# Seven-product units: eleven of the FFN's 22 input units instead of eight, in pairs, with the block sums kept in SBUF

## The reference

```
h = rmsnorm(x, norm_ffn)
gt, up = split(h @ w_ffn_in, 2)        # w_ffn_in: 1024 x 5632, D_FF = 2816
x = x + (silu(gt) * up) @ w_ffn_out    # w_ffn_out: 2816 x 1024
return rmsnorm(x, norm_final)
```

## Time and profile before

| | |
|---|---|
| time, median of three runs | 794.04 us (792.46 to 794.29) |
| the profiled execution's own time | 792.53 us |
| its span in the profile | 790.7 us |
| PE busy | 782.2 us, 99% |
| DVE, ACT, POOL busy | 457.6, 309.4, 105.3 us |
| TensorE clock granted | 0.998 of full speed |

### The profile page before, as it was taken

How to read it: one execution, slowest core, us unless ns; L and a number is a source line. 1 busy time by engine, 2 the same in 40 slices (tenths; PEclk the granted TensorE clock), 3 DMA queues, 4 the chain that set the end, 5 groups by cost and what they waited for, 6 DMA issues and landing times.

```text
span 790.7 us, 11974 instructions
## 1 busy us (share of the span) xinstructions
PE 782.2 (99%) x4670; PEld 666.1 (84%) x4670; DVE 457.6 (58%) x895; ACT 309.4 (39%) x552; POOL 105.3 (13%) x75
## 2 busy tenths in 40 slices
PE   9999999999999999999999999999999999999996
PEld 7878899889878787788888888999999998888885
DVE  5935432645766876657527698666666655422347
ACT  6212155243646566642316352333323323222235
POOL 1301000000000000002200671433333300000000
PEclk9999999999999999999999999999999999999999
DMA  7931345340311111145331533333333334222202
GB/s 236 346 121 54 107 93 148 73 122 4 108 54 54 54 54 42 41 146 145 134 109 75 139 106 107 107 106 106 106 106 105 93 127 155 106 107 106 106 1 106
DMA packets 101274, 83.32 MB, mean 105 GB/s; under 512 B 16960, under 2 KB 94832, under 8 KB 101232
## 3 DMA queue, kind: packets, MB, share of 16 engines
q1 hardware_dynamic: 100992, 82.46, 34.9%
q10 hardware_dynamic: 240, 0.29, 0.1%
HBM read 77.44 MB, written 5.29 MB: 105 GB/s over the span
## 4 chain that ended last, share of the span: by engine, by line
PE 98%; DMA 0%; ACT 0%; issue 0%; DVE 0%; ACTq 0%; DVEq 0%
PE bank L1699 28%; PE bank L1700 28%; PE bank L1701 28%; PE bank L1932 2%; PE bank L1951 2%; PE bank L1919 2%; PE bank L1833 1%; PE bank L1874 1%; PE bank L1855 1%; PE bank L1796 1%; PE bank L1740 1%; PE bank L1946 1%; PE bank L1746 0%; PE bank L1749 0%; PE bank L1723 0%; PE bank L1886 0%
## 5 line engine op out<-in xcount | busy, mean ns | idle before, releaser
L1023 DVE TENSOR_TENSOR w_lo<-w_raw,w_hi 128x2048 fp32r<-128x2048 f32 (+2 forms) x29 | 64.5, 2225 | 79.8 <-ACT w_hi L660 79.8
L1699 PE MATMUL bank<-n_hi,w_hi 128*128 128x512 f32 x272 | 108.8, 400 | 0.0
L1701 PE MATMUL bank<-n_hi,w_lo 128*128 128x512 f32 x272 | 106.1, 390 | 0.0
L1700 PE MATMUL bank<-n_lo,w_hi 128*128 128x512 f32 x272 | 106.0, 390 | 0.0
L1699 PE MATMUL bank<-h_hi,w_hi 128*128 128x512 f32 (+1 forms) x272 | 99.5, 366 | 0.8 <-issue 0.8
L1700 PE MATMUL bank<-h_lo,w_hi 128*128 128x512 f32 (+1 forms) x272 | 99.1, 364 | 0.0
L1701 PE MATMUL bank<-h_hi,w_lo 128*128 128x512 f32 (+1 forms) x272 | 99.0, 364 | 0.0
L660 ACT CAST w_hi<-w_raw 128x2048 fp32r<-128x2048 f32 (+2 forms) x29 | 53.6, 1848 | 61.8 <-PE bank L1701 51.0
L1699 PE MATMUL bank<-w_hi,a_hi 128*128 128x512 f32 (+1 forms) x180 | 69.2, 385 | 0.0
L1700 PE MATMUL bank<-w_lo,a_hi 128*128 128x512 f32 (+1 forms) x180 | 69.2, 384 | 0.0
L1701 PE MATMUL bank<-w_hi,a_lo 128*128 128x512 f32 (+1 forms) x180 | 69.2, 384 | 0.0
(11 more groups left out here) (287 smaller groups left out, 1598.8 us busy)
## 6 DMA issues: line engine op xcount, KB each, us to landing
w_raw<-in_w_ffn_in_dram SPq DMA_DIRECT2D x44, 512.0 KB, 5.1
w_raw<-in_w_in_dram SPq DMA_DIRECT2D x37, 512.0 KB, 4.8
w_raw<-in_w_ffn_out_dram SPq DMA_DIRECT2D x22, 512.0 KB, 3.7
w_raw<-in_w_out_dram SPq DMA_DIRECT2D x8, 512.0 KB, 3.7
w_raw<-in_w_in_dram SPq DMA_DIRECT2D x12, 256.0 KB, 4.5
xs<-in_x_dram SPq DMA_DIRECT2D x4, 512.0 KB, 4.9
wck_k<-in_w_ck_dram SPq DMA_DIRECT2D x1, 2048.0 KB, 11.9
wck_v<-in_w_cv_dram SPq DMA_DIRECT2D x1, 2048.0 KB, 13.6
```

What stands on the lines that cost most here:

```text
L1023: dve.tensor_tensor(wlo[u % 2][:, 0:n], raw[u % 2][:, 0:n], whi[u % 2][:, 0:n].bitcast(F32), ALU.subtract).then_inc(lo_done, 1)
L1699: pe.matmul(dst, w[0], x_[0], start=start, stop=False)
L1700: pe.matmul(dst, w[0], x_[1], start=False, stop=False)
L1701: return pe.matmul(dst, w[1], x_[0], start=False, stop=stop)
```

## The change

- Seven units are now 5, 6, 8, 9, 11, 12, 14, 15, 17, 18, 20: eleven in place of eight, two and then one plain unit, in both slots. The loops are written out, unit by unit; `sevens(u)` and `plains(u)` count what came before u, and `multiplied(u)` is the semaphore and count of "unit u has been multiplied".
- There are two sets of `wa`/`wa22` tiles and two `s7` tiles, one per slot. The `s7` tiles now lie where `wlo` of the same slot lies, and `slo7` overwrites `s7` in place. So POOL may write the sums of unit u only when PE is through with the low part of unit u - 2: all of it where u - 2 is plain, and product by product (M5, M6, M7) where it is a seven unit.
- Odd units use banks 4 to 7, even units 0 to 3. The tanh is written into the unit's first bank, and the `gate_mul` instruction reads it there.
- In a seven unit PE begins with the three products of plain blocks; then come the four of sums. One of the seven DVE additions (`early_sums`) and its bank change with this, and the last addition moves to the next unit's `scaled_gate`.
- The t sums on POOL begin after the low part of unit 2. The reload of x waits for the last of the eleven seven units. The output product begins with the tiles of banks 0 to 3.

The core of the diff:

```
-SEVEN_FROM = 5
-SEVEN_N = (FT - 1 - SEVEN_FROM) // 2
+SEVEN = (5, 6, 8, 9, 11, 12, 14, 15, 17, 18, 20)
...
-        s7 = at("weight_sums", [4, 4, P], G + 4608)
+        s7 = [at(f"weight_sums{j}", [4, 4, P], B + 4 * SLOT * (4 + j)) for j in range(2)]
...
+        def multiplied(u):
+
+            return (m_done, 7 * sevens(u) + 7) if u in SEVEN else (gu_ready, plains(u) + 2)
...
             pool.wait_ge(h_lo, 2 * TT)
-            pool.wait_ge(r_ready, 2)
+            pool.wait_ge(lo_done, U_IN + 3)
...
-            def weight_sums(i, begins=False):
-
-                pool.wait_ge(raw_full[1], i * 32 + raw_count(U_IN + SEVEN_FROM))
-                if not begins:
-                    pool.wait_ge(lo_done, i * 2 + (U_IN + SEVEN_FROM - 1))
...
+            for u in SEVEN:
+                k, s = sevens(u), u % 2
+                w = slot_view(raw, s, KC, 256)
+                pool.wait_ge(raw_full[s], raw_count(U_IN + u))
+                if u - 2 in SEVEN:
+                    pool.wait_ge(m_done, 7 * sevens(u - 2) + 5)
+                else:
+                    pool.wait_ge(*multiplied(u - 2))
+                pool.tensor_tensor(s7[s][:, 2], w[:, 0:4, 0:P], w[:, 0:4, P:256], ALU.subtract).then_inc(s_sums, 1)
+                if u - 2 in SEVEN:
+                    pool.wait_ge(m_done, 7 * sevens(u - 2) + 6)
+                pool.tensor_tensor(s7[s][:, 0], w[:, 0:4, P:256], w[:, 4:8, P:256], ALU.add).then_inc(s_sums, 1)
+                pool.wait_ge(s_sums, 4 * k + 2)
+                pool.tensor_tensor(s7[s][:, 1], s7[s][:, 0], w[:, 0:4, 0:P], ALU.subtract).then_inc(s_sums, 1)
+                pool.wait_ge(*multiplied(u - 2))
+                pool.wait_ge(s_sums, 4 * k + 3)
+                pool.tensor_tensor(s7[s][:, 3], w[:, 4:8, 0:P], s7[s][:, 1], ALU.subtract).then_inc(s_sums, 1)
...
+            def keep_m1(u):
+                k = sevens(u)
+                act.wait_ge(m_done, 7 * k + 1)
+                if k:
+                    act.wait_ge(u_sums, 7 * k - 5)
+                act.copy(m1s[:], ps[4 * (u % 2)][:, 0:256]).then_inc(m1_out, 1)
+
+            def tanh_gate(u):
+                s = u % 2
+                act.wait_ge(g_scaled, u + 1)
+                act.activation(ps[4 * s][:], gs[:, s, :], ACT.Tanh, scale=0.5).then_inc(gu_tanh, 1)
...
+            for u in range(4, FT):
+                if u + 1 in SEVEN:
+                    plain_hi(u + 1)
+                tanh_gate(u - 1)
+                if u in SEVEN:
+                    keep_m1(u)
+                if u + 1 in SEVEN:
+                    sums_hi(u + 1)
+                else:
+                    unit_hi(u + 1)
...
+            def early_sums(u):
+
+                k, a = sevens(u), 4 * (u % 2)
+                dve.wait_ge(m1_out, k + 1)
+                dve.wait_ge(m_done, 7 * k + 3)
+                dve.tensor_tensor(gs[:, u % 2, 0:256], ps[a][:, 256:512], m1s[:], ALU.add).then_inc(u_sums, 1)
+                dve.wait_ge(m_done, 7 * k + 4)
+                dve.tensor_tensor(u2s[:], ps[a + 1][:, 0:256], m1s[:], ALU.add).then_inc(u_sums, 1)
...
+            for u in range(4, FT):
+                scaled_gate(u - 1)
+                if u + 1 in SEVEN:
+                    plain_lo(u + 1)
+                gated(u - 1)
+                if u in SEVEN:
+                    early_sums(u)
+                if u + 1 in SEVEN:
+                    sums_lo(u + 1)
+                else:
+                    unit_lo(u + 1)
+                if u in SEVEN:
+                    late_sums(u)
...
+                pe.wait_ge(wa_lo, 2 * k + 2)
+                pe.wait_ge(gu_free, u + 1)
+                product(a, 0, plain(0, 4), turned(0, early))
+                pe.wait_ge(t_lo, 4)
+                product(a + 2, 256, [v[s][1][:] for v in (ahi7, alo7)], mixed(3))
+                pe.wait_ge(m1_out, k + 1)
+                product(a, 256, plain(4, 8), turned(4, early))
+                pe.wait_ge(hi_done, U_IN + u + 1)
+                pe.wait_ge(lo_done, U_IN + u + 1)
+                product(a + 1, 0, summed(1), mixed(1))
+                product(a + 2, 0, summed(2), mixed(2))
+                product(a + 3, 0, summed(0), mixed(0))
+                pe.wait_ge(u_sums, 7 * k + 2)
+                product(a + 1, 256, summed(3), turned(4, late))
```

More of the change, by code:

```diff
@@ L81, with sevens, plains @@
 HALVES_NSA = (4, 2)
+def sevens(u):
+    return sum(v < u for v in SEVEN)
+def plains(u):
+    return u - sevens(u)
 def schedule():
@@ L627, in _ @@
-            pool.tensor_tensor(t_f[:, 2], t_f[:, 2], l_f[:, first, late], ALU.subtract).then_inc(t_made, 1)
+            link(pool.tensor_tensor(t7[:, 2], h_f[:, second, late], h_f[:, first, late], ALU.subtract))
+            link(pool.tensor_tensor(t7[:, 2], t7[:, 2], l_f[:, second, late], ALU.add))
+            pool.tensor_tensor(t7[:, 2], t7[:, 2], l_f[:, first, late], ALU.subtract).then_inc(t_made, 1)
             pool.wait_ge(t_made, 1)
-            link(pool.tensor_tensor(t_f[:, 1], t_f[:, 2], h_f[:, first, early], ALU.add))
@@ L861, in _ @@
                     square_x2(t - 1)
[L864 to L873, removed]
@@ L910, in even_hi, with unit_hi @@
[L910 to L920 removed]
+            def unit_hi(u):
+                s = u % 2
+                act.wait_ge(raw_full[s], raw_count(U_IN + u))
+                if u >= 2:
+                    act.wait_ge(*multiplied(u - 2))
+                else:
+                    act.wait_ge(gu_ready, 1)
+                act.copy(whi[s][:, 0:2048], raw[s][:, 0:2048]).then_inc(hi_done, 1)
@@ new lines, in plain_hi, with sums_hi @@
+            def plain_hi(u):
+                s = u % 2
+                act.wait_ge(raw_full[s], raw_count(U_IN + u))
+                same = [v for v in SEVEN if v < u and v % 2 == s]
+                if same:
+                    act.wait_ge(m_done, 7 * sevens(same[-1]) + 3)
+                w = slot_view(raw, s, KC, 256)
+                act.copy(ahi7[s][0][:], w[:, :, 0:P]).then_inc(wa_hi, 1)
+                act.copy(ahi7[s][1][:], w[:, 4:8, P:256]).then_inc(wa_hi, 1)
+            def sums_hi(u):
+                s = u % 2
+                act.wait_ge(*multiplied(u - 2))
+                act.wait_ge(s_sums, 4 * sevens(u) + 4)
+                act.copy(shi7[s], s7[s][:]).then_inc(hi_done, 1)
@@ L952, in _ @@
-            seven_tanh(SEVEN_N - 1)
-            even_tanh(SEVEN_N - 1)
-            act.wait_ge(raw_full[0], raw_count(U_OUT))
-            act.wait_ge(gu_ready, SEVEN_N + SEVEN_FROM + 1)
-            act.copy(whi[0][:, 0:2048], raw[0][:, 0:2048]).then_inc(hi_done, 1)
+            unit_hi(2)
+            tanh_gate(0)
+            tanh_gate(1)
+            unit_hi(3)
+            act.wait_ge(x2_out, 16)
+            part_of_t(0, 2)
+            part_of_t(1, 1)
+            tanh_gate(2)
+            unit_hi(4)
@@ L959, in _ @@
-            act.activation(tg[:, 1, :], gs[:, 1, :], ACT.Tanh, scale=0.5).then_inc(gu_tanh, 1)
+            tanh_gate(FT - 1)
             act.wait_ge(gu_free, 24)
@@ L1551, in _ @@
+            unit_lo(1)
             dve.wait_ge(x2_ss, TT)
```

352 lines of the change are left out of this document (107 added, 245 removed).

## The result

The changed kernel takes 805.67 us (median of 4 runs, 804.54 to 807.55), the kernel before 793.29 beside it (792.46 to 794.29). The ratio is 1.0156, with a 95% interval of 1.0134 to 1.0178. The profiled execution took 806.16 us with a span of 804.4; that of before took 792.53 with 790.7.

A forecast was written before the change was run, and what follows sets the result against it. PE, busy 99% of the span, was taken as the bound. Terms -2.9 - 1.0 + 2.4 + 9.4 = +7.9 us gave 800.4 for the profiled execution, 801.9 against the median, range 798 to 806.

The forecast's parts named there:

- The mechanism of the stops: Ahead of a pair's second unit's third product, PE waits for ACT's M1 copy, queued behind tanh: 2.0 us.
- Three units fewer in plain form: On PE, three plain units become seven units, 10.90 to 9.93 us each: -2.9 us.
- The placement of tiles: In seven units, moved tiles change product times: taken as zero, bounds -3.6 to +1.8 us over eleven.
- Opening: Units 2 to 5: DVE unhindered in unit 2, -1.0 us; waits at unit 5 of 0.4 + 2.0, +2.4 us.
- Pairs: Second units of pairs: PE waits 2.0 us in each of four and 1.4 in 5/6: +9.4 us, bounds +3.5 to +14.
- Hidden: Other work, such as u2 additions, slot refills, x reload, output product and unrolled code, adds nothing to PE's time.
- R4: After 2 us stops TensorE drops to 1.2 GHz; 3 us at half speed after six stops, 9 us more: 811; 3%.
- R1: POOL and DVE block little: 0.7 us per pair, nothing at unit 5; -0.4 us, 793.6; 10%.
- R2: In pairs the three leading products cover the chain and PE never waits: -3.9 us, 790.1; 5%.
- R3: DVE leaves pairs late, blocking the next plain unit, or seven units take 10.1: over 3 us per pair, +15, 809; 8%.

The follow-up runs named there:

- the first experiment: The changed kernel with ACT's copy of M1 ahead of the previous unit's tanh in unit 5 and each pair's second unit: 790.83 us, ratio 0.9967.
- the alternating version: The changed kernel with the earlier kernel's eight seven units, 5, 7, ..., 19, no two in a row: 793.41 us, ratio 0.9999.
- the last three versions: The changed kernel with M1's copy ahead of tanh and DVE's plain-block cut behind early additions: 790.10 us; also with twelve seven units, 790.07, and thirteen, 792.93.
- the three edits together: The changed kernel with M1's copy ahead of tanh, plain blocks of 9, 12, 15, 18 cut earlier, and t_lo behind unit 3's gate: 791.12 us, ratio 0.9979.

## Why the forecast held, and the term it missed

The mechanism of the stops was right, and the time came within the range, 3.8 us above the forecast of 801.9. Against the 793.29 us of the kernel before beside it the change cost 12.4 us, where 7.9 was forecast: about a third of the loss is not in the sum. By its steps, for the profiled executions (806.16 against 792.53, +13.6 us where +7.9 was forecast):

1. Three units fewer in plain form: -2.9 forecast and measured (10.90 - 9.93 each). The placement of tiles was taken as nothing, with -3.6 to +1.8 as bounds; the six even seven units take 10.02, +0.5.
2. Opening. Unit 2 unhindered: -1.0 forecast, -1.06 measured (44.66 less the stop of 0.64, against 45.08). DVE was forecast through with t_lo at 482.2 and the gate of unit 3 begins at 482.23. The two stops were forecast at 0.4 and 2.0 and are 0.64 and 1.81. The sum is +2.4 forecast and measured. That the copy stands behind the tanh there too is shown by the first experiment, which removes this stop as well.
3. Pairs: 1.4 + 4 x 2.0 = 9.4 forecast; 1.15 + 1.98 + 2.01 + 1.98 + 2.01 = 9.1 measured. In the four later pairs the chain was forecast at 14.8 us and is 14.8, piece by piece. For the pair 5/6 the forecast gives 1.4 without its working, and the figures that it does show do not lead there: with 2.0 us of stop inside unit 5, PE wants the third product of unit 6 at 12.7 + 2.0 = 14.7, and a chain of 14.8 leaves 0.1. The 1.15 came because the chain was 16.0 us there: POOL's four sums took 8.5 us (486.29 to 494.79), blocked by DVE's low part of unit 5's sums (3.33) and its cut of unit 6's blocks (1.68 and 1.78). That the number was close is luck. The part of the 2.0 us stops that comes from blocking, 1.3, is shown by moving DVE's cut away. That the order makes the stops is shown twice, on ACT and on DVE.
4. Hidden: no stop ahead of M4 or M7, none in first units of pairs, none in unit 20, and the alternating version shows that the new code by itself, with odd seven units, costs nothing. Right.
5. The clock, rival R4. This is the term that was mis-sized. The forecast put it at nothing in its sum and gave it 3%, at 9 us (a stretch after each of six stops), since in the kernel before the clock stayed at 1.00 over a stop of 0.9. In fact half-clock stretches came behind three of the seven stops in the first trace and two in the second, of 1.6 us each: +4.9 in the profiled execution, a little over half of what R4 had. Another 0.5 us lies in the first matmuls behind the other stops, which start 0.19 to 0.23 apart in place of 0.12.

The sum: -2.9 + 0.5 - 1.06 + 2.45 + 9.13 + 4.9 + 0.5 = +13.5. Of the 5.7 us above the forecast's sum, 4.9 are the clock, 0.5 the tiles of the even units, 0.5 the slow first matmuls, and the stops take 0.3 back; 0.1 is not accounted for. PE's 4.2 us more of busy time are the same account: -2.9 + 0.5 + 4.9 + 0.5, and 1.0 because the trace counts PE as busy for the first 0.16 us of each stop, seven now and one before; together 4.0.

That the time still fell within the range is in part luck: the range was made wide for the opening, the pairs and the tiles, and the clock was to lie outside it.

R1 and R2 fell with POOL's sums at 6.66 us. R3's wait beyond 3 us did not come: PE stops in no plain unit. Its other half, seven units at 10.1, came true for the six even ones (10.02).

What stays open is why a stop is followed by half clock or not. The lengths of the stops don't tell it (2.18 with, 3.05 without, the same stop of unit 12 once with and once without). The profiles of the versions without the stops of 2 us in the pairs show no stretch, and none of their runs was granted less than 0.997, so the stretches came with those stops. They are not the only cause of a lower clock: one of 26 executions of the kernel before, beside the last three versions, was granted 0.947 and took 796.36 us.

## What to carry to other kernels

Write down the chain between two such units over all engines, and ask of each link whether it makes what is needed or only stands ahead of it in a queue: here swapping two instructions on ACT turned a ratio of 1.016 into 0.997. Price a forecast stop of TensorE of 2 us at more than its length, with a spread between executions: here seven stops of 11.6 us cost 5.4 us on top in one execution. Once a stop is gone, look for what the late engine owes next: the copy ahead of the tanh brought up a stop of 0.54 us elsewhere, and the three edits together one of 1.26.

## What the runs showed of the hardware

- Behind some stops of 2 to 3 us TensorE ran at 1.2 GHz for 3.2 to 3.6 us and lost about 1.6 us. The runs of the changed kernel lie between 804.5 and 807.6 us with clocks of 0.994 to 0.990, and those of the versions whose pairs stop for under 1.2 us have clocks of 0.997 and above.
- A seven unit takes 9.93 us in the odd slot and 10.02 in the even one, with the same products. Slot, banks and tiles differ together, and no run separates them.
- tanh of 128x512 written to a bank takes 0.60 us, where to SBUF it took 0.63; no run changes this alone.
- A blocked DVE or POOL instruction again ended at the other's end plus its own time less a little: POOL's second sum took 2.27 for 1.29 beside DVE's cut, and that took 1.88 for 1.22.
- Some profiles run late by up to 1.7 us before anything that is changed here: POOL's first t sum starts at 448.36 in the alternating version and at 446.67 in the changed kernel, and part of this is there in the first 10 us (two matmuls of L1696 take 1.05 us in place of 0.62). Unit starts of different kernels are therefore compared as differences.
